# Reversing the moving columns of the projections and starting their weight buffers 96 bytes later

## The reference, cut to what matters

```python
q, k, v = jnp.split(jnp.einsum('bsd,de->bse', h, w_in), 3, axis=-1)      # blocks 1 and 2: 1024 -> 3072
... attention (stick-breaking in block 1, differential in block 2) ...
x = x + jnp.einsum('bse,ed->bsd', o, w_out)                              # 1024 -> 1024
g = jnp.einsum('bsd,df->bsf', h, w_gate); u = jnp.einsum('bsd,df->bsf', h, w_up)   # 1024 -> 2816, twice
x = x + jnp.einsum('bsf,fd->bsd', jax.nn.silu(g) * u, w_down)            # 2816 -> 1024
# block 3: u @ w_in (pool, attention, state-space and gate columns), p_pool, p_attn, p_ssd, w_out,
# ffn_up, a causal convolution over three tokens, silu(g) * val, ffn_down, a last rmsnorm
```

## Time and profile before

| | |
|---|---|
| median of the runs | 2198.0 us |
| profiled execution, own time | 2196.64 us |
| its span, first to last instruction | 2194.9 us |
| PE busy | 2172.3 us (99%), 10146 matmuls |
| PE weight loads busy | 1728.5 us (79%) |
| DVE busy | 1374.2 us (63%) |
| ACT busy | 792.2 us (36%) |
| granted TensorE clock | 0.998 of full |

### The profile page before, as it was taken

How to read it: one execution, slowest core, us unless ns; L and a number is a source line. 1 busy time by engine, 2 the same in 40 slices (tenths; PEclk the granted TensorE clock), 3 DMA queues, 4 the chain that set the end, 5 groups by cost and what they waited for, 6 DMA issues and landing times.

```text
span 2194.9 us, 28356 instructions
## 1 busy us (share of the span) xinstructions
PE 2172.3 (99%) x10146; PEld 1728.5 (79%) x10146; DVE 1374.2 (63%) x2077; ACT 792.2 (36%) x1161; POOL 0.2 (0%) x4
## 2 busy tenths in 40 slices
PE   8999999999999999999999999999999999999998
PEld 6777788888887777888888877777788888888887
DVE  6666665554448887655554476677855567888733
ACT  5555432222235555322222224457622223222222
POOL 0000000000000000000000000000000000000000
PEclk9999999999999999999999999999999999999999
DMA  4211233333332222333333332222233333333332
GB/s 144 58 53 53 67 96 96 96 96 91 103 93 59 60 63 59 96 96 96 96 94 98 96 79 68 58 69 66 72 97 96 96 101 96 96 96 96 101 96 91
DMA packets 367107, 188.31 MB, mean 86 GB/s; under 512 B 8968, under 2 KB 366265, under 8 KB 367033
## 3 DMA queue, kind: packets, MB, share of 16 engines
q1 hardware_dynamic: 367033, 187.30, 29.9%
HBM read 185.18 MB, written 2.10 MB: 85 GB/s over the span
## 4 chain that ended last, share of the span: by engine, by line
PE 89%; DVE 6%; ACT 2%; issue 2%; DVEq 0%; ACTq 0%
PE lin L1802 78%; PE S L1867 1%; PE ob L1898 1%; PE S L1880 1%; DVE conv L1440 1%; PE ob L2014 1%; PE S L1979 1%; ACT w_hi L544 1%; PE lin L1828 1%; PE S L1828 1%; PE S L1885 1%; PE misc L1992 1%; ACT L826 0%; PE S L2145 0%; PE ob L2170 0%
## 5 line engine op out<-in xcount | busy, mean ns | idle before, releaser
L544 ACT ACTIVATE w_hi<-raw 128x1024 fp32r<-128x1024 f32 x361 | 381.4, 1057 | 835.4 <-PE lin L1802 806.8
L952 DVE TENSOR_TENSOR w_lo<-raw,w_hi 128x1024 fp32r<-128x1024 f32 x361 | 440.8, 1221 | 208.2 <-ACT w_hi L544 207.2
L1802 PE MATMUL lin<-h_hi,w_hi 128*128 128x512 f32 x1928 | 492.3, 397 | 0.4
L1802 PE MATMUL lin<-h_lo,w_hi 128*128 128x512 f32 x1928 | 481.8, 392 | 0.0
L1802 PE MATMUL lin<-h_hi,w_lo 128*128 128x512 f32 x1928 | 477.7, 390 | 0.0
L1802 PEld LDWEIGHTS lin<-h_hi,w_hi 128*128 128x128 f32 x1928 | 357.9, 188 | 86.7 <-issue 13.4
L1802 PEld LDWEIGHTS lin<-h_hi,w_lo 128*128 128x128 f32 x1928 | 361.1, 188 | 74.2
L1802 PEld LDWEIGHTS lin<-h_lo,w_hi 128*128 128x128 f32 x1928 | 358.9, 188 | 73.9 <-issue 0.5
L1802 PE MATMUL lin<-gu_lo,w_hi 128*128 128x512 f32 x528 | 131.4, 389 | 0.0
L1802 PE MATMUL lin<-gu_hi,w_hi 128*128 128x512 f32 x528 | 131.4, 389 | 0.0
L1802 PE MATMUL lin<-gu_hi,w_lo 128*128 128x512 f32 x528 | 131.4, 389 | 0.0
(11 more groups left out here) (388 smaller groups left out, 2173.2 us busy)
## 6 DMA issues: line engine op xcount, KB each, us to landing
raw<-in_w_in_dram SPq DMA_DIRECT2D x108, 512.0 KB, 3.8
raw<-in_w_gate_dram SPq DMA_DIRECT2D x44, 512.0 KB, 3.8
raw<-in_w_up_dram SPq DMA_DIRECT2D x44, 512.0 KB, 3.8
raw<-in_ffn_up_dram SPq DMA_DIRECT2D x44, 512.0 KB, 3.8
raw<-in_w_down_dram SPq DMA_DIRECT2D x32, 512.0 KB, 3.8
raw<-in_w_out_dram SPq DMA_DIRECT2D x24, 512.0 KB, 3.8
raw<-in_ffn_down_dram SPq DMA_DIRECT2D x16, 512.0 KB, 3.7
raw<-in_w_down_dram SPq DMA_DIRECT2D x16, 384.0 KB, 3.4
```

The lines of the kernel that those rows point to most:

```text
L544: act.activation(w_hi[u.slot][:, :, :], raw[u.slot][:, :, :], ACT.Copy).then_inc(hi_ready, 1)
L952: dve.tensor_tensor(w_lo[u.slot][:, :, :], raw[u.slot][:, :, :], w_hi[u.slot][:, :, :].bitcast(f32), ALU.subtract).then_inc(lo_ready, 1)
L1802: ins = pe.matmul(acc, (wh, wh, wl)[part][:, k, :], (hi, lo, hi)[part][:, k0 + k, :], start=first and part == 0 and k == 0, stop=last and ...
```

## The change

Two things change. The four weight buffers, and what lies between them and the arena, begin 96 bytes later, while `xT`, `h_hi`, `h_lo` and `raw` stay. In the three matmul calls of the projections the moving operand and the accumulator are both written with `[::-1]` along the tokens: the instruction reads column 511 first and column 0 last, and writes its results in the same order, so each token's sum still lands in its own column. The weights are read as before.

```diff
@@ -189,6 +189,7 @@
         raw = [fixed(f"raw{s}", [P, KT, P]) for s in range(2)]
+        top[0] += 96
         w_hi = [fixed(f"w_hi{s}", [P, KT, P], f32r) for s in range(2)]
         w_lo = [fixed(f"w_lo{s}", [P, KT, P], f32r) for s in range(2)]
@@ -1799,7 +1800,7 @@
-                        ins = pe.matmul(acc, (wh, wh, wl)[part][:, k, :], (hi, lo, hi)[part][:, k0 + k, :],
+                        ins = pe.matmul(acc[:, ::-1], (wh, wh, wl)[part][:, k, :], (hi, lo, hi)[part][:, k0 + k, ::-1],
@@ -1825,7 +1826,7 @@
-                        ins = pe.matmul(acc[:, :], (wh, wh, wl)[part][:, k, :], (o_hi, o_lo, o_hi)[part][:, k, :],
+                        ins = pe.matmul(acc[:, ::-1], (wh, wh, wl)[part][:, k, :], (o_hi, o_lo, o_hi)[part][:, k, ::-1],
@@ -1841,7 +1842,7 @@
-                    return pe.matmul(out_bank(l, f)[:, :], w_row, (o_hi, o_lo, o_hi)[part][:, k, :], start=False, stop=part == 1,
+                    return pe.matmul(out_bank(l, f)[:, ::-1], w_row, (o_hi, o_lo, o_hi)[part][:, k, ::-1], start=False, stop=part == 1,
```

## The result

The changed kernel takes 2243.63 us (median of 4 runs, 2242.92 to 2244.47) against 2197.96 us (4 runs): 1.0211 times as long, 95% interval 1.0199 to 1.0223. It was forecast to be faster. The time came out near the slow end of the range, on the side of rival B.

What follows compares the result with a forecast made beforehand. PE was taken to bound the kernel through the distance between projection matmul starts. 2196.64 - 41.6 us of excess won + 1 us lost in mixed stages = 2156.0; run median 1.4 us higher: 2157 us, range 2113 to 2247.

Steps and rivals of the forecast that it cites:

- rival B: Projections: present layout may be the favourable settled pattern; the change makes matmuls slower, up to 2246 us; chance 0.25.
- What bounds the kernel: Whole kernel: PE busy 99%; time is the number of projection matmuls, 8328, times the 226.67 ns between their starts.
- The excess of 13.3 ns: Each projection matmul: time beyond its columns' 213.3 ns; 111 us over 8328 matmuls, all that the change can shrink.
- 3.3 ns as what must stay: Least excess per matmul, read from the half-rate full float32 matmuls of L2014; leaves 10.0 ns each, 83.3 us, to win.
- Turning one stream around changes how often they meet: Projections: reversal changes how often weight and moving reads meet; taken as a gain of 5.0 ns each, 41.6 us.
- upper bound: Projections at the exponent matmuls' 232.5 ns, the full-rate limit: 5.8 ns more each, a loss of 48.3 us.
- Rival A: Projections: excess is a fixed charge per weight load whatever address or direction; no effect, 2198 us; chance 0.18.
- Rival C: Projections: reversed operand or accumulator drops the stream to half rate, 3891 us; chance 0.09.
- Rival D: Projections: reads no longer disturb each other, nearly all the excess goes, 2115 us; chance within the 0.48 for faster.
- feeding: Weight load and rounding for projections: 3.05 us a unit against 5.32 us of matmuls, so it stays hidden.
- the loss of gain in mixed stages: Differential attention and two other mixed stages: part of the gain becomes waiting; 1 us taken.
- 0 for the tables: Exponent matmuls: `exact` moves from 288 to 384 bytes past a multiple of 512; under 2 us either way, 0 taken.

## Why the prediction was wrong, step by step

*What bounds the kernel* was right: no wait was added, the other engines only waited longer, and the loss is the distance between matmul starts times their number. It was read from the right rows, and the long pieces of the chain carried the verdict as said.

*The excess of 13.3 ns, and 3.3 ns as what must stay.* The first is a measurement. Reading the remaining 10.0 ns as a cost of weight reads, to be had back, is the step that failed, and with it the term of the sum: 5.0 ns won on each of 8328 matmuls, 41.6 us, measured as 6.7 ns lost in the long pieces and 45.7 us lost in all. Half the reads made the distance larger (230.0 ns) and eight columns less left it alone (226.7 ns). In 18 experiments none came below 226.7, so the lower end of the range rested on a gain that no layout tried gives.

*"Turning one stream around changes how often they meet", with the sign taken from the room.* That the address and order of the two reads matter is shown: the direction alone, the offset alone, the moving operand alone and the common shift all say so. The sign was argued from the fact that there was more room below (10.0 ns) than above (5.8 ns). That isn't evidence for a direction. The rows that were evidence spoke the other way: the exponent matmuls, whose weights lay 32 bytes past a multiple of 256, ran at 232.5 ns, and the table above has 233.3 ns for projections at 32 bytes. That row was named as the upper bound and as rival B's price, and held against it was that the four stand "after other work". They stand right behind projection matmuls, whose last five before them took 1.16 us (from 115.76), and the run with 224 bytes shows that their address made the difference. It was the better forecast.

*Rival B* was the mechanism. Its price, 5.8 ns on 8328 matmuls or 48 us, stands against 45.7 us measured. The agreement is partly luck: in the long pieces it was 6.7 ns, in the mixed stages less. There 8328 - 5788 = 2540 matmuls lost 47.6 - 38.6 = 9.0 us of span, 3.5 ns each. Its account of the earlier trace rows, that a stream settles into a pattern and is slower until it has, is seen in the starts (231, 236, 228, 232, 231, then 227 ns), but it is the small part of the 0.11 us: the first distance, 314 ns, is 87 above 226.7, and the five behind it together 25. The word "settle" is right also in that more than one pattern can be had. Why the aligned layout settles lower isn't shown by any run.

*Rival A* (a fixed charge) is refuted by the offset alone. *Rival C* (half rate) is refuted by every reversed run, and for the accumulator by its own. *Rival D* wasn't seen.

*The other terms*: feeding stayed hidden, the loss of gain in mixed stages didn't arise, and the exponent group took 0.93 us at its new offset too, so 0 for the tables was right there; by the table that is luck of the two offsets, 32 and 128 bytes past a multiple of 256, which are both slow. The 3.3 ns of the half-rate group holds up start by start: inside it the distances are 430 ns for 512 columns, 322 for 384, 216 for 256 and 109 for 128, which leaves 2.0 to 3.3 ns each. The sum of 2.16 us gave it only because a long first distance (512 ns) and a short last one (31 ns) nearly cancel. The allocator `fixed`, which the text ahead places at line 174, stands at line 182.

*Still open* is what holds the distance. The settled distances 226.7, 233.3 and 240.0 ns are 34, 35 and 36 times 6.67 ns, the time of 16 columns at 2.4 GHz. The others fit in whole patterns: 236.7 ns are 71 steps for two matmuls, 228.9 are 103 for three, 232.4 are 244 for seven. In the trace of the offset alone the distances most often repeat as 234, 235, 233, 232, 237, 238, 231 ns, in all 1640 ns for seven matmuls, 246 steps; with half the weights 236, 229, 224, 227, 234, 230, in all 1380 ns for six, 207 steps. In the changed kernel most starts alternate 231 and 236 ns, 467 ns or 70 steps, where the direction alone gives an even 233 and 234. This is what a stream would do that meets something with a beat of 6.67 ns in the path to SBUF and repeats only in step with it. No run isolates such a thing, so it is a description and not a shown cause.

## What to carry to other kernels

Where long runs of one kind of matmul bound a kernel, divide a long piece of the chain by its count and compare with the columns' own time; then look for the same kind of matmul in other layouts in the same trace, and forecast from that row, not from the room to the ideal. Keep float32r weights and moving operands at a distance that is a multiple of 256 bytes and read the moving columns in ascending order within 256 bytes: here anything else that was tried cost 1.0 to 3.4% of each such matmul in the first long piece. "Anything else" is the seven other offsets below 256 bytes and a fully reversed order, at 128 weight columns and 512 moving ones. It can come from one buffer's size further up in the list of allocations.

## What the runs showed of the hardware that was not expected

- A fixed distance of two buffers in SBUF, and nothing else, moved the time by 2.4% (2250.53 against 2197.64 us), and a common shift of both by nothing (2197.0 against 2196.5 us). Two kinds of matmul show the same rule: projections at 256 bytes and exponents at 512 run at 226.7 ns.
- Fewer weights can be slower: 64 instead of 128 weight columns took a float32r matmul from 226.7 to 230.0 ns. Fewer columns can be no faster: 504 and 512 take the same 226.7 ns.
- One layout can run at several paces: 233.3, 236.7 and 240.0 ns in different stretches of one execution, each kept for 1108 to 1560 matmuls.
- The best pace isn't there at once: after short matmuls the aligned stream ran at 228 to 236 ns for five matmuls before it came to 226.7.
- Reversed PSUM accumulators are free (2196.82 us against 2197.64).
